# A hybrid attention block on one core: the queue order of the attention turns, of the modulation pieces and of the gate pieces

## The reference

```
mod = silu(c) @ w_ada + b_ada                 # six vectors sh1, sc1, g1, sh2, sc2, g2 of 1024
h = rms_norm(x, norm1_g) * (1 + sc1) + sh1
q, k, v, u = split(h @ w_in)                  # 512, 128, 128, 512 columns
q, k = rope(rms_norm(q)), rope(rms_norm(k))   # per head of 64, rope on the first 16
attn = sliding-window attention (window 128, 8 heads, 2 kv heads, a sink per head)
pool = (trailing means of u over 2, 4, 8, 16 tokens - u) @ pool_w * pool_scale
x = x + g1 * (concat[attn, pool] @ w_o)
h2 = rms_norm(x, norm2_g) * (1 + sc2) + sh2
out = x + g2 * (relu(h2 @ w_mlp_in)^2 @ w_mlp_out)     # 4096 hidden units
```

## Time and profile before

| | |
|---|---|
| three runs | 960.61, 961.12, 961.18 us (median 961.12) |
| profiled execution | 960.62 us, its span 958.9 us |
| busy: PE, PE weight loads | 924.7 us (96%), 766.1 us (80%) |
| busy: DVE, ACT, POOL | 653.8 us (68%), 492.3 us (51%), 355.2 us (37%) |
| granted TensorE clock, mean | 0.998 of full |
| chain that ended last | PE 85%, DVE 6%, ACT 5%, DMA 2%, issue 2% |

### The profile page before, as it was taken

How to read it: one execution, slowest core, us unless ns; L and a number is a source line. 1 busy time by engine, 2 the same in 40 slices (tenths; PEclk the granted TensorE clock), 3 DMA queues, 4 the chain that set the end, 5 groups by cost and what they waited for, 6 DMA issues and landing times.

```text
span 958.9 us, 12636 instructions
## 1 busy us (share of the span) xinstructions
PE 924.7 (96%) x4413; PEld 766.1 (80%) x4413; DVE 653.8 (68%) x997; ACT 492.3 (51%) x874; POOL 355.2 (37%) x342
## 2 busy tenths in 40 slices
PE   2998999998999999999999999999999999999998
PEld 2887788886878888788887888888888888888887
DVE  6977887868544597655566545545786666779896
ACT  2657777777555553645544554455433544333331
POOL 8151122226132444988888878851000000000000
PEclk9999999999999999999999999999999999999999
DMA  9941432225122241754465444448998737997773
GB/s 357 365 160 45 132 111 88 90 66 170 51 88 88 89 153 44 248 192 157 162 194 184 171 143 143 164 149 287 350 329 301 262 91 237 312 311 246 236 247 110
DMA packets 92271, 175.54 MB, mean 183 GB/s; under 512 B 9320, under 2 KB 26288, under 8 KB 92208
## 3 DMA queue, kind: packets, MB, share of 16 engines
q1 hardware_dynamic: 92096, 174.70, 54.2%
q10 hardware_dynamic: 112, 0.04, 0.0%
HBM read 136.95 MB, written 37.75 MB: 182 GB/s over the span
## 4 chain that ended last, share of the span: by engine, by line
PE 85%; DVE 6%; ACT 5%; DMA 2%; issue 2%; POOL 0%; SPq 0%; DVEq 0%; ACTq 0%
PE psum L1967 26%; PE psum L1969 26%; PE psum L1968 26%; PE psum L1963 3%; DMA raw<-in_w_ada 2%; ACT probs L777 2%; PE psum L2046 1%; PE psum L2069 1%; ACT probs L785 1%; PE psum L2096 1%; PE psum L2027 1%; PE psum L2025 1%; PE psum L2024 1%; ACT qT L796 1%; DVE probs L1294 1%
## 5 line engine op out<-in xcount | busy, mean ns | idle before, releaser
L1075 ACT CAST down_operands<-down_raw 128x1024 fp32r<-128x1024 f32 x96 | 100.8, 1055 | 152.9 <-PE psum L1969 62.9
L1967 PE MATMUL psum<-down_operands 128*128 128x512 f32 x448 | 174.3, 389 | 0.0
L1968 PE MATMUL psum<-down_operands 128*128 128x512 f32 x448 | 174.3, 389 | 0.0
L1969 PE MATMUL psum<-down_operands 128*128 128x512 f32 x448 | 174.3, 389 | 0.0
L1702 DVE TENSOR_TENSOR down_operands<-down_raw,down_operands 128x1024 fp32r<-128x1024 f32 x93 | 112.5, 1220 | 16.2 <-ACT down_operands L1075 15.6
L1967 PE MATMUL psum<-h2T,w_operands 128*128 128x512 f32 x272 | 107.4, 395 | 1.9 <-DVE act_quads_a L1646 1.3
L1969 PE MATMUL psum<-h2T,w_operands 128*128 128x512 f32 x272 | 105.9, 390 | 0.0
L1968 PE MATMUL psum<-h2T,w_operands 128*128 128x512 f32 x272 | 105.9, 389 | 0.0
L1919 POOL TENSOR_TENSOR w_operands<-raw,w_operands 128x512 fp32r<-128x512 f32 x56 | 83.3, 1488 | 42.0 <-ACT w_operands L1027 42.0
L1968 PEld LDWEIGHTS psum<-down_operands 128*128 128x128 f32 x448 | 84.1, 188 | 17.6
L1969 PEld LDWEIGHTS psum<-down_operands 128*128 128x128 f32 x448 | 84.1, 188 | 17.4
(11 more groups left out here) (251 smaller groups left out, 1976.2 us busy)
## 6 DMA issues: line engine op xcount, KB each, us to landing
down_raw<-in_w_mlp_out SPq DMA_DIRECT2D x160, 256.0 KB, 4.4
down_raw<-act_scratch SPq DMA_DIRECT2D x112, 256.0 KB, 3.4
raw<-in_w_ada SPq DMA_DIRECT2D x32, 512.0 KB, 4.7
raw<-in_w_mlp_in SPq DMA_DIRECT2D x32, 512.0 KB, 4.8
act_scratch<-act_quads_a SPq DMA_DIRECT2D x64, 256.0 KB, 2.3
act_scratch<-act_quads_b SPq DMA_DIRECT2D x48, 256.0 KB, 3.5
slots<-in_w_ada SPq DMA_DIRECT2D x8, 512.0 KB, 10.4
xh<-in_x SPq DMA_DIRECT2D x8, 512.0 KB, 6.5
```

Source lines behind the costliest of these rows:

```text
L1075: nc.scalar.copy(o[:, 0, :, :], r[:, 0:2, :]).then_inc(op2_hi, 1)
L1967: mm(o, wh, ah, start=first, stop=False, skip_group_check=adds)
L1968: mm(o, wh, al, start=False, stop=False, skip_group_check=adds)
L1969: return mm(o, wl, ah, start=False, stop=last, skip_group_check=adds)
```

## The change

No operation is added or removed; the sums, the sizes and the DMAs are the same. What changes is where instructions stand in the queues:

- TensorE: in turn 2 `turn_x(3)` goes ahead of `score(0, 1)`; in turns 3 and 5 `turn_sums` goes ahead of `project_u(t)`; in turn 7 `pool_out(7)` goes ahead of `score(6, 0)`.
- ScalarE: in turns 3 to 7 `scale_x` and `normalise(t-2, 0)` go ahead of `hi_qk(t-1)` and `exps(t-2, 1)`, and `square_q(t)` ahead of the second `normalise`; turn 2 has an order of its own, with `hi_qk(1)` behind `hi_pT(0, 0)`; `hi_wo(0)`, `hi_mix(0, 0)`, `hi_wo(1)` and `keep_attn(5, 1)` change places around the end of the loop.
- VectorE: the pieces get three tables, for behind `maxes(t-2, 0)`, behind `dens(t-2, 0)`, and around `lo_qk(t-1)` and `dens(t-2, 1)`; `gain_q(t)` goes behind `lo_pT(t-2, 0)`; in turn 2 `lo_qk(1)` goes behind both. `lo_wo(0)` moves from GpSimd to VectorE.
- MLP: `add_g2` moves from the end of a block to behind U2 of the next; the last operation of `sum_head(1)` moves from ahead of U3 to behind C22 of block 2.

```diff
-        WO_POOL, WO_DVE = (0, 5, 6), (1, 2, 3, 4, 7)
+        WO_POOL, WO_DVE = (5, 6), (0, 1, 2, 3, 4, 7)
...  ScalarE, loop for t in 2..7
-                if t >= 3:
+                if t == 2:
+                    exps(0, 1)
+                    normalise(0, 0)
+                    normalise(0, 1)
+                    hi_pT(0, 0)
+                    hi_qk(1)
+                    square_q(t)
+                else:
                     keep_u(t)
-                if t >= 3:
-                    hi_qk(t - 1)
-                exps(t - 2, 1)
-                if 3 <= t and t + 1 < NT:
-                    scale_x(t + 1)
-                normalise(t - 2, 0)
-                square_q(t)
-                if t == 2:
-                    hi_qk(1)
-                normalise(t - 2, 1)
-                hi_pT(t - 2, 0)
+                    if t + 1 < NT:
+                        scale_x(t + 1)
+                    normalise(t - 2, 0)
+                    hi_qk(t - 1)
+                    exps(t - 2, 1)
+                    if t + 1 < NT:
+                        square_q(t)
+                    normalise(t - 2, 1)
+                    hi_pT(t - 2, 0)
...  VectorE, tables and loop
-            early_pieces = ([], [], range(4, 6), [], range(11, 13), range(15, 16), range(18, 20), range(22, 24))
-            late_pieces = (range(0, 4), [], range(6, 8), range(8, 11), range(13, 15), range(16, 18), range(20, 22), [])
+            first_pieces = ([], [], (5, 6), (8,), (12, 13), (16,), (18, 19), (22,))
+            between_pieces = ([], [], [], (9,), (14,), (17,), (20,), (23,))
+            late_pieces = ((0, 1, 2, 3), (4,), (7,), (10, 11), (15,), [], (21,), [])
...
-                dens(t - 2, 0)
-                maxes(t - 2, 1)
+                add_job_pieces(first_pieces[t])
                 if t == 2:
+                    maxes(0, 1)
+                    dens(0, 0)
                     make_h(3, 0)
                     make_h(3, 1)
                     dens(0, 1)
-                    lo_qk(1)
-                else:
+                    add_job_pieces(late_pieces[2])
+                else:
+                    dens(t - 2, 0)
+                    add_job_pieces(between_pieces[t])
+                    maxes(t - 2, 1)
+                    add_job_pieces(late_pieces[t][:1])
                     lo_qk(t - 1)
                     dens(t - 2, 1)
-                    add_job_pieces(late_pieces[t])
+                    add_job_pieces(late_pieces[t][1:])
...
-                gain_q(t)
                 lo_pT(t - 2, 0)
+                if t == 2:
+                    lo_qk(1)
+                gain_q(t)
...  mix_block
                 if b == HEAD:
-                    sum_head(1)
+                    sum_head_first(1)
+                if HEAD < b <= HEAD + KD:
+                    add_g2(b - HEAD - 1)
                 dve.wait_ge(up_done, up_count(b, "P7"))
...
                 v.tensor_tensor(act_quad("A22"), bank(o + 2), u3, ALU.add).then_inc(up_mixed, 1)
+                if b == HEAD:
+                    sum_head_last(1)
+                    dve.wait_ge(head_mixed, 8)
...
-                if b < HEAD + KD:
-                    add_g2(b - HEAD)
...  TensorE, loop for t in 2..7
-                if t >= 3:
-                    project_u(t)
                 if t in (3, 5):
                     ...
                     turn_sums(banks(1), acc).then_inc(mod_turned, 1)
+                if t >= 3:
+                    project_u(t)
+                else:
+                    pe.wait_ge(carry_kept, 2)
+                    turn_x(3)
                 score(t - 2, 1)
...
                 attend(t - 2, 1)
+                if t == NT - 1:
+                    pool_out(t)
                 pe.wait_ge(qk_lo, t)
                 score(t - 1, 0)
-                pool_out(t)
+                if t + 1 < NT:
+                    pool_out(t)
```

More of the change, by code:

```diff
@@ L899, in _ @@
                 if t == NT - 1:
+                    hi_wo(0)
+                hi_pT(t - 2, 1)
+                if t == NT - 1:
                     hi_mix(0, 0)
-                hi_pT(t - 2, 1)
                 keep_attn(t - 2, 0)
@@ L905, in _ @@
                     hi_h(t + 1, 1)
-                else:
[L907 to L910, removed]
+                keep_pooled(t)
+                if t + 1 < NT:
+                    keep_attn(t - 2, 1)
+                else:
+                    hi_wo(1)
             def square_x2(i):
@@ L968, in _ @@
             keep_pout(NT - 1)
+            keep_attn(NT - 3, 1)
             hi_wo(2)
@@ L1405, in _ @@
             norm_k(1)
+            add_job_pieces(late_pieces[1])
             add_carry(1)
@@ L1427, in _ @@
                     dens(0, 1)
-                    lo_qk(1)
+                    add_job_pieces(late_pieces[2])
                 else:
+                    dens(t - 2, 0)
+                    add_job_pieces(between_pieces[t])
+                    maxes(t - 2, 1)
+                    add_job_pieces(late_pieces[t][:1])
                     lo_qk(t - 1)
                     dens(t - 2, 1)
-                    add_job_pieces(late_pieces[t])
+                    add_job_pieces(late_pieces[t][1:])
                 if 3 <= t and t + 1 < NT:
                     make_h(t + 1, 0)
+                lo_pT(t - 2, 0)
+                if t == 2:
+                    lo_qk(1)
                 gain_q(t)
-                lo_pT(t - 2, 0)
                 if 3 <= t and t + 1 < NT:
@@ L1440, in _ @@
                 if t == NT - 1:
-                    lo_mix(0, 0)
+                    lo_wo(0)
                 lo_pT(t - 2, 1)
@@ L1447, in _ @@
                     lo_h(t + 1, 1)
+                else:
+                    lo_mix(0, 0)
+                norm_k(t)
                 if t == NT - 1:
                     lo_wo(1)
-                norm_k(t)
-                if t == 2:
-                    add_job_pieces(late_pieces[2])
             def make_h2_half(i):
@@ L1491, in _ @@
             dens(NT - 2, 0)
+            lo_mix(0, 1)
             maxes(NT - 2, 1)
-            lo_mix(0, 1)
             lo_wo(4)
@@ L1581, in lo_h2_last, with sum_head_first @@
                                 f32(h2T[:, NT - 1, 0, 4 * h:4 * h + 4, :]), ALU.subtract).then_inc(h2_lo_last, 1)
-            def sum_head(b):
+            def sum_head_first(b):
                 dve.wait_ge(head_kept, 4 * b + 4)
@@ L1593, in sum_head, with sum_head_last @@
                 v.tensor_tensor(act_quad("S2"), act_quad("S1"), act_quad("A11"), ALU.subtract).then_inc(head_mixed, 1)
+            def sum_head_last(b):
                 if b == 1:
@@ L1622, in _ @@
             lo_t3(4)
-            sum_head(0)
+            sum_head_first(0)
+            sum_head_last(0)
             def mixed(b, name):
@@ L2151, in _ @@
                     pe.wait_ge(mod_taken, t // 2 + 1)
-                if t == 2:
-                    pe.wait_ge(carry_kept, 2)
-                    turn_x(3)
-                else:
+                if t >= 3:
                     turn_qk(t - 1)
```

6 lines of the change are left out of this document (2 added, 4 removed).

## The result

The changed kernel takes 946.22 us (median of 5 runs, 945.89 to 946.76), the kernel before, run beside it, 961.18 us: ratio 0.9842, 95% interval 0.9829 to 0.9856. It is 15.0 us faster. I had said 948.6 us, 946.5 to 953.5.

What follows compares the result with a forecast made beforehand. TensorE's work plus its stalls was taken as the bound. Terms of 5.6 + 2.1 + 1.6 + 1.5 + 2.3 = 13.1 us, cut to 12.5, gave 948.1 profiled, 948.6 us as median; range 946.5 to 953.5.

Steps and rivals of the forecast that it cites:

- turn 2: Attention loop's turn 2: three TensorE stalls costing 3.3 us, 1.2 us of waits left, 2.1 us gained.
- turns 3 to 7: Attention loop: ten TensorE stalls, 3.2 us idle, all removed for a gain of 5.6 us.
- way out: End of the attention loop: TensorE reaches the first output product earlier; gain 1.6 us, bounds 0 and 4.9.
- head products and gate pieces: MLP: P3's wait for C22 goes, 1.5 us; P7's waits for U2 go in seven blocks, 2.3 us.
- taken off for thin margins: Turns and way out: six times 0.1 us deducted from the summed gain, 13.1 to 12.5 us.
- half stall: Turn 2's second stall, 0.52 us idle: said to shrink by half, since make_h(3) is reached at about the same time.
- wait of turn_x for lo_qk or of turn_p for lo_pT: Turns 3 to 6: such TensorE waits would show the forecast wrong; margins there were put at 0.3 to 0.6 us.
- price of a stall: TensorE: each stall costs its idle time plus 0.24 us, read from matmul starts around an up block's short stall.
- 22 stalls: TensorE stalls said to be removed: 10 in turns 3 to 7, 3, 1 and 8 in the MLP.
- ScalarE's order: Turns 3 to 7: scale_x and first normalise earlier hide stalls on x's scaled row (0.4 us) and normalised probabilities (1.8 us).
- the reduction behind it is hidden: Turns 3 and 5: turn_sums ahead of project_u's 5.5 us of matmuls hides the reduction, removing two stalls, 0.7 us.
- slower rival: Attention loop: VectorE's pieces asked for before their loads land, up to 23.5 us lost, 972 us; chance 0.05.

Runs made afterwards that it cites:

- b3: Kernel before with only turn 2's new order, on TensorE, ScalarE and VectorE with its pieces; 957.79 us, ratio 0.9967.
- a3: Changed kernel with the MLP edits (add_g2 and the head sums) undone, leaving the attention part alone; 950.15 us, ratio 0.9896.
- d2: Kernel before with the new orders of turns 2 to 7, way out and MLP as before; 952.48 us, ratio 0.9914.
- b4: Kernel before with only the way out of the loop as in the changed kernel; 958.84 us, ratio 0.9979.
- e1: Changed kernel with make_h2_half(1) ahead of lo_mix(3, 0), turn_x2(0, 1) behind tile 2's first output product, root_x2(1) ahead of normalise_last(7, 1); 944.03 us, ratio 0.9819.
- c2: Changed kernel with 896 of add_g2's 1024 columns put back ahead of U2; 948.15 us, ratio 0.9865.
- b1: Kernel before with only ScalarE's new order in turns 3 to 7; 966.74 us, ratio 1.0056.
- a4: Kernel before with only turn_sums moved ahead of the u product in turns 3 and 5; 969.20 us, ratio 1.0088.
- b2: Kernel before with VectorE's new order in turns 3 to 7 and turn_sums moved, turn 2's pieces and ScalarE as before; 965.13 us, ratio 1.0046.
- d1: Kernel before with the new orders of turns 3 to 7 on ScalarE, VectorE and TensorE, turn 2 and way out as before; 960.61 us, ratio 0.9993.
- c4: Changed kernel with all of add_g2 put back ahead of U2, cut into eight operations; 1007.74 us, ratio 1.0480.
- d3: Changed kernel with lo_mix(0, 1) ahead of dens(6, 0) and w_o_lo(5) moved from GpSimd to VectorE behind w_o_lo(4); 948.05 us, ratio 0.9869.

## Why the prediction was right in kind and short in size

What failed is the size of two steps of the sum, not the mechanism. Turn 2 was put at 2.1 us and gave 2.8 (traces) to 3.0 (b3), and 0.6 us was taken off for margins that held. With them the attention part was worth 10.7 us (a3) and not the 8.7 that were left of 5.6 + 2.1 + 1.6, and the time fell below the range.

The traces' column is the difference of the two kernels: turns 3 to 6 in the table above 5.58, turn 7 to turn_p(5, 1) 0.59, less 0.37 that b3 shows to be turn 2's; the way out from there to the last output product of tile 0 (212.38 to 235.63 us before, 204.50 to 225.94 after); the MLP from 295.02 to 583.04 and from 285.22 to 569.19.

| term | predicted | by the traces | by the runs |
|---|---|---|---|
| turns 3 to 7 | 5.6 | 5.8 | 5.2 (b3 to d2), 5.8 (a3 less b3 and b4) |
| turn 2 | 2.1 | 2.8 (2.44 and 0.37 in turn 3) | 3.0 |
| way out | 1.6 | 1.8 | 1.95 |
| head products and gate pieces | 1.5 + 2.3 | 4.05 | 1.7 + 2.3 |
| taken off for thin margins | -0.6 | 0 | not run by itself |

The 5.2 of b3 to d2 may be low by what d2's fallen clock cost behind the loop (some 1.6 us in its profiled execution).

- **Turn 2 is the term that was mis-sized most.** I had written "I set 1.2 us against 3.3 and keep 2.1": a half stall left at the second place, 0.4 us at pool_windows(2) and 0.5 at attend(0, 1). The half stall isn't there, and the two waits are 0.21 and 0.16 us. The places were right, the sizes two to three times too large.
- **The discount for thin margins failed.** In turns 3 to 6 no wait of turn_x for lo_qk or of turn_p for lo_pT appears. Margins of 0.3 to 0.6 us held.
- **The price of a stall was a little low**, and it was asked of the wrong stalls: 0.27 instead of 0.24 us on each of 22 stalls would be 0.7 us, and stalls without shown idle weren't counted. The 0.27 was read at the up blocks alone; the three stalls that e1 took away fit 0.24. In turn 4 the k and v product started at 135.11 us and turn_p behind it at 138.23, 3.12 us later; in the changed kernel 130.56 and 133.51, 2.95. That 0.17 us with no idle, once a turn, fits c2's 0.23, though no run took it away by itself.
- **Turns 3 to 7: the sum was right, its account was not.** I credited ScalarE's order with L785 and L709, and turn_sums with L1414 because "the reduction behind it is hidden", without asking when the pieces ahead of it are ready. By themselves these edits lose 5.9 and 8.3 us (b1, a4). They pay only with VectorE's pieces moved, those of turn 2 included (b2, d1, d2). The change moves them too, so that the sum came out is in part luck. My condition for the slower rival, a piece that isn't ready when TensorE asks, was the right danger, with VectorE's order and not the DMA as its cause.
- **The way out, head products and gate pieces** came out within 0.4 us of their terms, and the MLP was additive to the rest (a3).
- **The range** began at the whole 13.1 us "and a little". The table adds to 14.5 us by the traces, and the medians lie 15.0 apart. Each term had been cut on the safe side, so the low end had no room; I should have added the errors of both signs around the undiscounted sum. The rest of 0.5 us I can't place: before the loop, in code that isn't changed, profiled runs differ more than that (the first pool_out between 60.8 and 64.0 us). The clock may have a part in it, which is not shown for these runs: of 70 executions of the kernel before beside the experiments, 14 had a mean granted clock of 0.996 and took 961.96 us (median), 28 had 0.998 and took 960.73.

## What to carry to other kernels

Price a stall of a pipelined engine by the spacing of its starts, not by the idle time, and look for spacings above the normal one where no idle shows. When an edit makes an engine ask earlier, walk back through everything that it asks for, on every engine, including what was ready with room to spare before; orders that are tuned together can lose apart and win together, so test them in groups. Don't discount a forecast for margins that the arithmetic says hold: put them into the range.

## What the runs showed of the hardware

- **Two engines that take turns.** add_g2 (128 x 1024) lasts 2.31 us ahead of U2 and 1.43 us behind it in the changed kernel. In c4 eight operations of 128 columns last 7.29 us. A 128 x 4 operation of VectorE lasts 2.29 us beside GpSimd's w_o_lo (d3) and 0.16 elsewhere. It goes the other way too: GpSimd's root on 128 x 10 takes 1.96 us in the turns before, and 2.88 in turn 7 of the changed kernel, where it starts beside VectorE's w_o_lo(0). The Trainium skill (SBUF — State Buffer, SBUF: two separate sides) describes the port pair that the two engines share as an exclusive lock that an operation holds for its whole length. The traces agree: d3's operation ends with GpSimd's. They add its price where work is cut: the same columns take 2.31 us in one piece and 7.29 in eight, five of which wait for a turn of GpSimd.
- **Stalls that cost without showing.** 0.23 us lost a block for no idle, 0.36 for 0.09 (c2, before).
- **The clock falls behind stalls, and not only behind long ones.** After 2.65 us of idle (b1) the granted clock stayed 1.00; after 3.49 (a4) it was 0.57 over the next 3.7 us, and after 5.06 (c4) 0.50 over 4.4 us, with starts 0.43 us apart instead of 0.23. The 1.55 us of turn 2 before left it at 1.00. But behind d2's two waits of 1.13 and 0.72 us it fell to 0.50 for 3.4 us, and behind the same two in the kernel before it did not: the length of one stall does not decide alone, and what does is open.
